# A hybrid block (RWKV-7, differential attention, hierarchical experts): the recurrence's small products spread over four quarters of the array, joints between stages rearranged, and identity products placed where TensorE has nothing to do

## What is computed

```python
def step(state, inp):
    r_t, w_t, k_t, v_t, kk_t, a_t = inp
    sa = jnp.einsum('bhvk,bhk->bhv', state, -kk_t)
    state = (state * w_t[:, :, None, :]
             + sa[..., None] * (kk_t * a_t)[:, :, None, :]
             + v_t[..., None] * k_t[:, :, None, :])
    return state, jnp.einsum('bhvk,bhk->bhv', state, r_t)
...
_, y = lax.scan(step, s0, tuple(map(seq_first, (r, decay, k, v, kk, a))))
y = jnp.moveaxis(y, 0, 1)
mean = jnp.mean(y, axis=-1, keepdims=True)
var = jnp.mean(jnp.square(y - mean), axis=-1, keepdims=True)
yn = ((y - mean) * lax.rsqrt(var + RWKV_GN_EPS)).reshape(bsz, length, RWKV_WIDTH)
```

## Time and profile before

| | before |
|---|---|
| median of 3 runs | 2782.72 us (2782.28 to 2785.11) |
| profiled execution | 2786.39 us |
| its span | 2784.5 us |
| its mean granted clock | 0.973 |
| PE busy | 2571.4 us, 92% |
| DVE, ACT, POOL busy | 1561.2, 1315.8, 316.7 us |
| PE in the recurrence, 1220 to 1765 us | 510.7 of 545 us |

### The profile page before, as it was taken

One profiled execution on the slowest core, in us unless ns is written; L12 is line 12 of the kernel. 1 busy time (PEld: TensorE's weight loads), 2 busy tenths in 40 slices (PEclk: granted clock), 3 DMA queues, 4 the chain that ended last, 5 costly groups with the idle time before them and its releaser, 6 DMA issues. The chain is left out here.

```text
span 2784.5 us, 65171 instructions
## 1 busy us (share of the span) xinstructions
PE 2571.4 (92%) x27593; PEld 2141.3 (77%) x27593; DVE 1561.2 (56%) x2370; ACT 1315.8 (47%) x2266; POOL 316.7 (11%) x367
## 2 busy tenths in 40 slices
PE   6999999999989999989999999899895999999992
PEld 6989896777766766679999889778784888888882
DVE  4566664443035555544444444553326888888884
ACT  5655542222134444334444444462223777777771
POOL 0121222332000000001212222100001000000002
PEclk9999999999999999999999999999996999999996
DMA  4443342222122323212222201244355999999976
GB/s 110 156 164 137 131 148 72 92 92 74 40 94 66 101 63 130 86 46 80 55 61 58 58 21 33 77 114 136 118 187 212 392 392 396 398 391 393 398 298 257
DMA packets 162645, 440.46 MB, mean 158 GB/s; under 512 B 16295, under 2 KB 96825, under 8 KB 150097
## 3 DMA queue, kind: packets, MB, share of 16 engines
q1 hardware_dynamic: 146413, 381.95, 38.5%
q10 hardware_dynamic: 9060, 29.56, 2.8%
q0 software_dynamic: 6912, 25.17, 2.4%
HBM read 344.22 MB, written 92.41 MB: 157 GB/s over the span
## 5 line engine op out<-in xcount | busy, mean ns | idle before, releaser
L2610 DVE TENSOR_TENSOR ex_wL<-wx,ex_wH 128x2048 fp32r<-128x2048 f32 x192 | 436.0, 2285 | 46.6 <-ACT ex_wH L2514 44.8
L2514 ACT CAST ex_wH<-wx 128x2048 fp32r<-128x2048 f32 x192 | 366.4, 1911 | 94.3 <-PE ex_bank L2410 70.9
L2408 PE MATMUL ex_bank<-ex_wH,ex_xTH 128*128 128x512 f32 x512 | 200.5, 392 | 2.4 <-DVE ex_xTL L2615 2.4
L2409 PE MATMUL ex_bank<-ex_wH,ex_xTL 128*128 128x512 f32 x512 | 200.1, 391 | 0.0
L2410 PE MATMUL ex_bank<-ex_wL,ex_xTH 128*128 128x512 f32 x512 | 200.1, 391 | 0.0
L709 PE MATMUL ph_acc<-ph_wH,uH 128*104 128x512 f32 x480 | 192.5, 401 | 6.5 <-DVE ph_wL L721 6.5
L709 PE MATMUL ph_acc<-ph_wH,uL 128*104 128x512 f32 x480 | 189.5, 395 | 0.0
L709 PE MATMUL ph_acc<-ph_wL,uH 128*104 128x512 f32 x480 | 189.4, 395 | 0.0
L413 PE MATMUL pf_acc<-uH,pf_wH 128*128 128x348 f32 x648 | 160.3, 356 | 6.4 <-DVE pf_wL L533 6.4
L413 PE MATMUL pf_acc<-uL,pf_wH 128*128 128x348 f32 x648 | 138.6, 322 | 0.0
L413 PE MATMUL pf_acc<-uH,pf_wL 128*128 128x348 f32 x648 | 138.3, 322 | 0.0
(11 more groups left out here) (397 smaller groups left out, 6782.0 us busy)
## 6 DMA issues: line engine op xcount, KB each, us to landing
wx<-in_expert_w_gate SPq DMA_DIRECT2D x32, 2048.0 KB
wx<-in_expert_w_up SPq DMA_DIRECT2D x32, 2048.0 KB
wx<-in_expert_w_down SPq DMA_DIRECT2D x32, 2048.0 KB
s_y<-ex_y ACTq DMA_DIRECT2D x32, 512.0 KB, 10.1
fw<-in_w_in SPq DMA_DIRECT2D x27, 512.0 KB
hw<-in_w_in SPq DMA_DIRECT2D x6, 2048.0 KB, 10.1
s_qkT<-ph_stg ACTq DMA_DIRECT2D x4, 2080.0 KB, 6.9
mb_gt<-s_pT SPq DMA_DIRECT2D x16, 512.0 KB, 3.5
```

Source lines behind the costliest of these rows:

```text
L2408: nc.tensor.matmul(out, aH, bH, start=first, stop=False)
L2409: nc.tensor.matmul(out, aL, bH, start=False, stop=False)
L2514: nc.scalar.copy(wH[:, w, part], raw(j, s)[:, part]).then_inc(w_high, 1)
L2610: nc.vector.tensor_tensor(wL[:, w, part], raw(j, s)[:, part], wH[:, w, part], ALU.subtract).then_inc(w_low, 1)
```

## The change

**Four quarters.** `across(e, h)` gives h for e = 0 and 1 - h for e = 1, and `row(e, h)` is the token half by it: the second head pair has its token side on the other partition half. Products that lead from channels to tokens or back (`masked`, `raw`, which was `solve` 2, `tokens`, the state's part of q = 1, the new state, and the old state's part of Y, now an item of its own, `old_state`) therefore use the four quarters in turn, one for each head. The outputs of e = 0 and e = 1 go to different banks (0 and 1, or 6 and 7). Products of tokens by tokens (`solve`, q = 2, q = 3, most of Y) stay on two. `masked`, `raw`, `tokens`, `old_state` and the group norm's transposes share banks 0 and 1, and each of them waits, by `after_reading`, until the one before has been read.

**Who computes R and Y.** The product of masked inputs and v for the next chunk (L1526) is issued with q = 2. ACT copies both results at once (`RA`, 256 wide). R is then one DVE instruction from the bank and `RA`. Y is now a DVE addition of the bank and `Hs`, ACT's copy of the old state's part, where ACT copied Y before. `Nn` has four buffers. `seq` has four pieces, so a round has 8 slots, and `SPREAD` is rewritten to that.

**Joints.** The first cast and subtraction of `attention` and of `output_and_route` are done in four parts each, and PE waits for a part. In `attention` the first gate products come ahead of the wait for `consts`. In `merge_branches` the first `y_split` on DVE is in two halves; `load_w(2)` comes ahead of the loop and the loop issues `load_w(q + 3)`; ACT's square comes ahead of the two gates; each `wo_split` comes one unit earlier. The recurrence's layer-norm rows are loaded by four DMAs where one was (8 become 32), since two heads' rows no longer stand together, and `load_branch` and `load_rest` use `across` for their rows.

**Identity products.** `keep_awake(n)` issues n products of the identity with itself, 128 by 128 in fp32, into a bank part that nothing reads. They stand at the end of the projections' programs (16, 16), at the start of `project_heads` (8), around `attention` (6, 12), at the recurrence's end (5), around the merge (24, 14), at the start of `output_and_route` (8) and in its tail (6, 3, 6), and in the experts' start ahead of the ranking (40), behind it (42), ahead of the first `turn_x` (26) and of the first `gate` (8). Those at a stage's end wait for its last results first.

```diff
+def keep_awake(nc, c, out, n):
+
+    for _ in range(n):
+        nc.tensor.matmul(out, c.ident[:], c.ident[:], start=True, stop=True)
...
+            pe.wait_ge(evicted, LASTG + OPEN)
+            keep_awake(nc, c, acc[:, 1 - LASTG % 2, 0, 0:128], 16)
...
+                    if x == 0 and step % 6 == 0:
+                        pe.wait_ge(first_low, step // 6 + 1 + OPEN)
...
+            keep_awake(nc, c, bank[:, 0:128], 6)
+            fill(FIRST)
...
+def across(e, h):
+
+    return h if e == 0 else 1 - h
...
-            return (first(2) + late(9) + tokens(A) + piece()
-                    + first(6) + late(10) + ahead(A + 2, 0) + piece()
-                    + first(7) + late(11) + ahead(A + 2, 1) + piece()
-                    + first(8) + late(12) + piece() + piece()
-                    + first(9) + second(2) + tokens(B) + piece()
-                    + second(6) + first(10) + ahead(B + 2, 0) + piece()
-                    + first(11) + second(7) + ahead(B + 2, 1) + piece()
-                    + first(12) + second(8) + piece() + piece())
-
-        SPREAD = {"sum0": 0, "sum1": 1, "mean": 2, "sub": 2, "sq": 3, "var0": 8, "var1": 9, "std": 11, "rin": 12, "nrm": 12,
-                  "t0": 17, "e0": 17, "t1": 18, "e1": 18, "t2": 24, "e2": 24, "add": 25, "gate": 25}
+            old_state = lambda ch: [("h", ch)] if old and ch % NCH > 0 else []
+            return (tokens(A) + first(6) + late(10) + piece() + old_state(A - 2)
+                    + first(7) + raw(B) + late(11) + piece()
+                    + first(8) + late(12) + piece()
+                    + ahead(A + 2) + first(9) + piece()
+                    + tokens(B) + second(6) + first(10) + piece() + old_state(B - 2)
+                    + second(7) + raw(A + 2) + first(11) + piece()
+                    + second(8) + first(12) + piece()
+                    + ahead(B + 2) + second(9) + piece())
...
+            def after_reading(*then):
+                for x in last_read:
+                    pe.wait_ge(*x)
+                last_read[:] = [then]
...
+                    for e, h in PAIRS:
+                        last = mm(bank[row(e, h), e, 2 * j * TC:(2 * j + 2) * TC].rearrange("p (a t) -> p a t", a=2),
                                   BK[z][half(h), e, j, cols], KR[z][half(h), e, :, cols], start=True, stop=True)
...
+            def raw(ch):
+                d, z, cols = place(ch)
+                after_reading(n_read, ch + 1 + OPEN)
+                for e, h in PAIRS:
+                    last = mm(bank[row(e, h), e, 0:TC], KR[z][half(h), e, 0, cols], BK[z][half(h), e, 0, cols], start=True, stop=True)
...
+                        last = mm(bank[row(e, h), e, j * RD:(j + 1) * RD], src, c.ident[half(h), half(h)], start=True, stop=True)
...
+                        pe.wait_ge(y_done, ch + OPEN)
+                        pe.wait_ge(seq_dve, added(ch - 1))
+                        for e, h in PAIRS:
+                            last = mm(bank[row(e, h), 6 + e, 384:384 + RD], KR[z][half(h), e, 0, cols], S[half(h), t % 2, e, :], start=True, stop=True)
+                elif q == 2:
                     if ch > 0:
-                        pe.wait_ge(seq_act, 4 * ch + OPEN)
-                    if t > 0:
-                        pe.wait_ge(seq_dve, added(ch - 1))
+                        pe.wait_ge(y_done, ch + OPEN)
+                    pe.wait_ge(rest_done, ch + 1 + OPEN)
+                    for e, h in PAIRS:
+                        last = mm(o(1, e, h), Qf[row(e, h), s, e, :], R[row(e, h), e, :], start=True, stop=True)
+                    if ch + 1 < NC:
+                        pe.wait_ge(tok_read, ch + 2 + OPEN)
+                        pe.wait_ge(m_read, ch + 2 + OPEN)
+                        for e, h in PAIRS:
+                            last = mm(o(2, e, h), M4[row(e, h), (ch + 1) % MS, e, 2, :], tok[row(e, h), (ch + 1) % TS4, 2, e, :], start=True, stop=True)
+                elif q == 3:
+                    pe.wait_ge(*at_dve(ch, 12))
+                    pe.wait_ge(seq_act, 2 * ch + 1 + OPEN)
+                    for e, h in PAIRS:
+                        last = mm(o(0, e, h), Gf[row(e, h), s, e, :], RA[row(e, h), 0, e, :], start=True, stop=True)
...
+                    pe.wait_ge(seq_act, 2 * ch + 2 + OPEN)
+                    if t < NCH - 1:
+                        for j, right in ((0, lambda e, h: Uu[row(e, h), e, :]), (1, vv)):
+                            for e, h in PAIRS:
+                                mm(bank[half(h), 6 + e, 128:128 + RD], tok[row(e, h), s, j, e, :], right(e, h), start=(j == 0), stop=(j == 1))
...
+            def old_state(ch):
+                d, z, cols = place(ch)
+                after_reading(h_read, carried(ch))
+                for e, h in PAIRS:
+                    last = mm(bank[row(e, h), e, 0:RD], KR[z][half(h), e, 1, cols], S[half(h), ch % NCH % 2, e, :], start=True, stop=True)
+                last.then_inc(h_done, 1)
...
+            keep_awake(nc, c, bank[:, 1, 256:384], 5)
...
+                    nc.scalar.copy(RA[0:PX, 0:n], bank[0:PX, 6, 128:128 + 128 * n].rearrange("p (k e d) -> p k e d", k=n, e=2)).then_inc(seq_act, 1)
...
+            def old_state(ch):
+                act.wait_ge(h_done, carried(ch))
+                act.wait_ge(y_done, ch + OPEN)
+                nc.scalar.copy(Hs[0:PX], bank[0:PX, 0:2, 0:RD]).then_inc(h_read, 1)
...
+                        nc.vector.scalar_tensor_tensor(out=R[0:PX], in0=bank[0:PX, 6:8, 384:384 + RD], scalar=-1.0, in1=RA[0:PX, 1],
+                                                       op0=ALU.mult, op1=ALU.subtract).then_inc(rest_done, 1)
...
+                        tt(Y[x][0:PX, at:at + 2, :], out(2), Hs[0:PX], ALU.add).then_inc(y_done, 1)
...
+            load_w(2)
             for q in range(NU):
-                if q + 2 < NU:
-                    load_w(q + 2)
+                if q + 3 < NU:
+                    load_w(q + 3)
...
+                for q in range(2):
+                    pe.wait_ge(w_low, q + 1 + OPEN)
+                    for n in range(2):
+                        if q == 0:
+                            pe.wait_ge(y_half, n + 1 + OPEN)
+                        rows(q, 0, (n,))
...
+            keep_awake(nc, c, bank[:, 7, 0:128], 24)
...
+            pe.wait_ge(o_low, NS + OPEN)
+            keep_awake(nc, c, bank[:, 7, 0:128], 14)
...
+                if q == KD:
+                    wo_split(0)
+                if KD <= q < NU - 1:
+                    wo_split(q - KD + 1)
...
+            keep_awake(nc, c, bank[:, 7, 0:128], 8)
...
+            keep_awake(nc, c, bank[:, 7, 0:128], 6)
...
+            keep_awake(nc, c, bank[:, UP_BANK, 0:128], 40)
             pe.wait_ge(o_ready, 1 + OPEN)
...
+            keep_awake(nc, c, bank[:, UP_BANK, 0:128], 42)
...
+            keep_awake(nc, c, bank[:, UP_BANK, 0:128], 26)
             turn_x(pe, 0, 0, 0)
+            keep_awake(nc, c, bank[:, UP_BANK, 0:128], 8)
             gate(pe, 0, 0, 0, 0)
```

293 lines of the change are left out of this document (153 added, 140 removed).

## The result

The changed kernel takes 2774.16 us (median; 2769.64 to 2777.96), the kernel before 2785.24 us over the runs that were made beside it. The ratio is 0.9961, with an interval of 0.9951 to 0.9971: 11 us less, where the forecast had 36. The profiled execution is the fastest of the changed kernel's (2769.64 us, span 2767.8); against the profiled execution of before it is 16.7 us shorter, so a third of the difference between the two traces is luck of the draw.

A forecast was written before the change was run, and what follows sets the result against it. PE's instruction stream, with waits for instruction packets, was taken to bound the recurrence. Outside it -24.4 us and inside -12 made -36.4: profiled 2786.4 to 2750, less 3.7 over the median, gave 2746 us; range 2702 to 2778.

The forecast's parts named there:

- What bounds the recurrence: Recurrence: PE's stream sets the time, with an instruction packet every 4.01 us, 1.4 us before the request and 2.6 after.
- only the first is certain to shrink: Recurrence: of each packet cycle, the 1.4 us of work before the request shrinks to 1.1; the other 2.6 stays.
- the 41 us that the cycle was to give: Recurrence: about 136 packets, each cycle 0.3 us shorter (3.7 for 4.0), make 41 us less before new waits.
- The new waits: Recurrence: PE waits for shared banks and copies, 0.7 us a chunk, up to 56 us; net recurrence forecast -12 us.
- The merge: Inside the merge: earlier weight loads remove PE's wait, -6.2 us, and half clock behind it, -1.8: together -8.
- The start of the merge: Start of the merge: DVE's subtraction in halves, -1 us, and the clock, -2: together -3.
- The clock 6.1 us at half, -3.0: Start of the attention: 6.1 us run at half clock, which full clock would shorten by 3.0 us.
- The experts' start: Routing's tail and experts' start: products at full instead of half clock, together -8.6 us, of which -2.4 in the tail.
- The second: Rival, recurrence: the four quarters do not run beside each other; +17 us there, 2775 us in all; chance 0.10.
- The third: Rival, recurrence: sharing rows costs more than taking turns, crossed products losing load overlap; +45 us, 2803 in all; chance 0.08.
- The first: Rival, recurrence: instruction loading follows the pace, waits behind packets not growing; -56 us, 2702 in all; chance 0.14.
- the fourth: Rival, joints: the clock is not held, identity products run at half clock and are not hidden; 2779 us; chance 0.08.

The follow-up runs named there:

- the run with two quarters: The changed kernel with the second head pair's token side back on its own half, so all products use two quarters; order and waits kept: 2783.46 us, ratio 0.9997.
- wide products in step 7: The changed kernel with the solve's 12 products of step 7 streaming 104 columns instead of 52, no instruction more: 2782.45 us, ratio 0.9998.
- the run with transposes: The kernel before with 6 of 12 token products in each chunk of the recurrence done as transposes: 2903.04 us, ratio 1.0433.

## Why the prediction was wrong

**What bounds the recurrence** was read rightly, and the surprise is how far it goes. Packets pace PE. The forecast put two thirds of the effect of less work into the 2.6 us behind a request and one third, 1.4 to 1.1 us, on the path. That step, "only the first is certain to shrink", failed: the part ahead of the request stayed at 1.43 us. By the trace it now holds 118 instructions where it held 104; at the forecast's pace these alone take 1.3 us. So the 41 us that the cycle was to give are the term that failed: PE is faster per instruction, by about what was forecast, and packets still come once in 4 us. The runs with 41 and 98 us of added work that cost 8 and 9 us say the same from the other end: the price is 0.1 to 0.2 of the work, where the cycle as drawn has 0.4 (41 of 98). Part of that gap is not the cycle's: with added work fewer waits stay open (42 us of them in the changed kernel, 30 to 31 in these two) and the clock falls less often. Why a request comes later in instructions when PE has stood longer behind the one before is not settled.

**The new waits** were priced at up to 56 us with -12 us as a middle between -41 and +15. The measured value of the recurrence's part is +5 us (alone) to +8 (in the changed surroundings), inside the bounds but on the other side of nothing. The runs divide it: quarters -9, order and waits +18. The forecast allowed 29 us for open waits (-41 to -12). Measured by starts as above, the time lost other than behind packets grew by 27 us, but most of that falls between a request and its packet's restart, where it costs nothing, as the forecast had said: the part ahead of a request has 0.08 us of it in a cycle for 0.03, some 7 us in the stage. The allowance was too large, not too small, and so it is not what turned the sign. Two of its lengths were misread, too: 12 matmuls are 24 records, 0.57 us by the earlier trace rows and 0.58 in the changed kernel, not 0.29, and 20 matmuls are some 0.85 us, not 0.6. The waits named are there; waits of PE in the changed kernel, 1220 to 1762 us:

```profile
PE rw_bank L1428 <- ACT rw_H L1610: 5.5, 19, 1.7
```

This is `raw` behind ACT's copy of `Hs`, as forecast, 19 times; it counts only idle time beyond the modelled end of the record before, so it is less than the 13 us by starts. Two things were not in the sum. First, the stage's beginning, which stays at half clock for longer. PEclk there, before and in the changed kernel:

```profile
1211.00:1217.90 6.90, 6.11 (x90) 5.69 (x92) 2.43 (x5) 1.01 (x4) 0.81 (x2) 0.50 0.01 2
1212.00:1225.70 13.70, 10.49 (x240) 9.36 (x242) 4.40 (x14) 2.78 (x8) 1.21 (x3) 0.50 0.01 2
```

The 300th product record comes 16.1 us after the first (before 14.5), in the run with two quarters 18.6; in the other runs with the changed recurrence it is 14.5 to 16.8, in the others with the old one, transposes apart, 14.2 to 14.8. Second, the clock further on. Before, no stretch inside the recurrence behind 1217.9 had it at half. The changed kernel has two of 3.4 us, and the six other runs with four quarters and no column added to the solve's products have 3 to 6. One such stretch and the same length behind it, in the changed kernel:

```profile
1317.90:1321.30 3.40, 3.40 (x88) 3.40 (x85) 1.36 (x5) 0.88 (x3) 0.11 (x1) 0.50 0.27 73
1321.30:1324.70 3.40, 3.14 (x143) 2.98 (x138) 1.74 (x9) 1.81 (x7) 0.40 (x1) 1.00 0.30 73
```

88 records for 143, so a stretch costs about 1.3 us at most; two to six of them are 3 to 8 us. With the old recurrence (before and three runs that have it) there is none; with wide products in step 7 there is none and with two quarters in the new order one: where PE got its work back, the clock held. That PE's idle time behind packets is what brings the clock down is a reading and not shown: the run with transposes has 19 such drops and hardly a wait behind a packet. What the start, the drops and the waits leave of the +5 to +8 us is not traced to a cause.

**The merge** was the good step: -8 for the loads and the cold stretch behind them, and the run with this edit alone gave -7.7 to -8.6. The start of the merge was forecast at -3. Its first own product came 3.8 us later than before, and with the clock's gain in, at the 31st product record, it was still 2.0 us behind, because 24 identity products were taken as hidden and are not: the prediction compared the counts of the experts' start with the idle times there and did not do so at the other joints. Eight ahead of the heads, six ahead of the attention and eight ahead of the output hold PE in the same way: the first own product comes 0.9, 1.2 and 1.9 us later behind the stage before than in the run without them. "The clock 6.1 us at half, -3.0" at the attention came about half: the row above has 0.50 for 3.4 us there despite 22 identity products around the joint. By the 31st record the joints ahead of the heads, the attention and the output gave -1.3, -1.0 and -2.4 us, where -2.2, -4.7 and -4.4 were forecast ahead of the third taken off.

**The experts' start** behaved as drawn. Rows of the changed kernel that answer to the earlier trace rows:

```profile
2079.98 1.95 PE L2268 MATMUL or_bank<-or_wr,or_uT 128*128 128x36 f32 x16 [0.49 <-issue]
...
2107.62 2.21 PE L2567 MATMUL ex_bank<-ex_wL 128*128 128x48 f32 x16 [0.75 <-DVE ex_wL L2800]
...
2117.19 1.05 PE L2517 MATMUL ex_bank<-ident,ex_x 128*128 128x128 f32 x8
```

1.95 for 3.60, 2.21 for 3.61, 1.05 for 1.97. The sum of it is 5.7 us in the trace, and only 3 in the medians of the run that has these alone.

**The sum.** By runs: joints and identity products -19 us where -24.4 was forecast; of these the loads 8, the identity products 8 and, by difference, the rest 3. The recurrence +8 where -12 was forecast. The first of these terms was mis-sized by a fifth, the second had the wrong sign, and it makes 20 of the 25 us between the forecast change of -36.4 and the measured -11.

**The rivals.** The second, that the quarters do not run together, is refuted by the starts. The third, that sharing rows costs more, is refuted by the same rows. With it falls the rule that was weighed, the Trainium skill's "TensorE: Matmul & The Clock Gate", Part 3, that a weight load overlaps products in flight only if its row group differs: here crossed pairs follow diagonal ones at 7 ns between starts, and eight records take 0.11 us. The first, that loading follows the pace, is refuted by the cycle of 3.96 us. Of the fourth, that the clock is not held, the part on identity products that run at half clock and hold PE is real, ahead of the merge and of the ranking. The range's upper end, 2778, holds the measured 2774; what fell outside is the size of the gain.

## What to carry to other kernels

Where a straight-line stage issues small products faster than its instructions can be brought in, count instructions, not columns: here each added PE instruction cost 15.6 ns for hardly any work, and 98 us of array work bought 9. Before work is taken off the engine that looks busiest, add some with the instruction count held (a wider product), and add empty instructions: two runs tell which of the two is the price. Put one run of the old part in the new surroundings early: here it would have shown that the heart of the change costs time. And a load issued one turn earlier, read off one long wait in the trace, was worth about as much as the four quarters.

## What the runs showed of the hardware

- Four 64 by 64 quarters with separate banks run beside each other in fp32 at twice the rate of two (0.11 to 0.12 us for 0.22 to 0.23 per eight records of 64 columns).
- A packet of 250 PE instructions came once in 3.95 to 4.04 us in the recurrence of thirteen kernels whose PE work there differed by up to a fifth, and PE's restart stood 2.5 to 2.6 us behind the packet in each. Where PE was slower still (the run with transposes) it was once in 5.0 us.
- PE's transposes and its ordinary products, alternating on different quarters, do not overlap: 0.17 to 0.24 us at each change.
- Inside the recurrence the granted clock fell to 0.50 for 3.4 us at a time: 2 to 6 times in seven kernels with four quarters, though no single wait of the changed kernel there is longer than 1.7 us, and 19 times in the one with transposes; in the four others with the old recurrence never.
